# Second layer's heads: value products between pieces of projection, clamps and scalings on ScalarE

## What is computed

```
q, k, v, o, g, z = split(h @ w_in)              # per head: q, k 128 wide, v, o, z 256 wide
order = tril(ones)                              # a step sees itself and what came before
dmat  = where(order, b[t] - b[s] + ig[s], -inf) # b: running sum of log(sigmoid(forget gate))
m_t   = max over s of dmat (and of the state carried in)
s     = (q @ k.T) * exp(dmat - m_t)             # weights of one head, one direction
num, den = s @ v, sum(s)                        # and the state's part
h     = num / max(|den|, exp(-m_t))             # forward h + backward h
y     = rmsnorm(sigmoid(o) * (h_f + h_b)) * hn * silu(z)
out   = y @ w_out
```

## Time and profile before

| | |
|---|---|
| median of 3 runs | 2987.71 us (2981.6 to 2988.95) |
| profiled execution | 2990.57 us, its span 2988.8 us |
| granted TensorE clock, mean | 0.996 |
| TensorE busy | 2932.5 us, 98% |
| VectorE busy | 2090.1 us, 70% |
| ScalarE busy | 1178.0 us, 39% |
| GpSimd busy | 103.5 us, 3% |

### The profile page before, as it was taken

The page is one execution under the profiler, slowest core; times in us unless marked ns, Lnnn a source line. Parts: engine busy times, 40 slices in busy tenths (PEclk is TensorE's granted clock), DMA queues, the critical chain, the costliest instruction groups (busy, mean ns, idle before and its releaser), DMA issues.

```text
span 2988.8 us, 43582 instructions
## 1 busy us (share of the span) xinstructions
PE 2932.5 (98%) x17098; PEld 2353.5 (79%) x17098; DVE 2090.1 (70%) x3957; ACT 1178.0 (39%) x2056; POOL 103.5 (3%) x188
## 2 busy tenths in 40 slices
PE   8999999999999999999999999999999999999999
PEld 7777778888888888878888888888888888885346
DVE  4576876788888776677666886677675678765455
ACT  4322323322332232242245555455444445543344
POOL 0000000000000000000000000000010120000000
PEclk9999999999999999999999999999999999999999
DMA  9777784354555455538636774645576443487997
GB/s 366 281 266 286 273 282 149 127 169 148 190 168 177 162 183 169 179 128 275 235 117 206 258 241 142 197 148 180 195 236 218 141 164 128 152 274 259 403 404 314
DMA packets 193197, 641.69 MB, mean 215 GB/s; under 512 B 21488, under 2 KB 36192, under 8 KB 192992
## 3 DMA queue, kind: packets, MB, share of 16 engines
q1 hardware_dynamic: 132080, 423.44, 40.6%
q10 hardware_dynamic: 58032, 207.12, 20.3%
q0 software_dynamic: 2880, 8.35, 0.9%
HBM read 624.15 MB, written 12.58 MB: 213 GB/s over the span
## 4 chain that ended last, share of the span: by engine, by line
PE 87%; DVE 7%; ACT 3%; DMA 2%; issue 1%; SPq 0%; DVEq 0%; ACTq 0%; POOL 0%; POOLq 0%
PE PS L506 15%; PE PS L502 11%; PE PS L504 9%; PE PS L505 9%; PE PS L635 7%; PE PS L637 7%; PE PS L636 7%; PE PS L1061 2%; PE PS L798 2%; PE PS L1472 2%; DMA AR<-e_w 1%; DVE WL L2389 1%; PE PS L1441 1%; PE PS L1428 1%; PE PS L1122 1%
## 5 line engine op out<-in xcount | busy, mean ns | idle before, releaser
L2389 DVE TENSOR_TENSOR WL<-WR,WH 128x1024 fp32r<-128x1024 f32 (+1 forms) x566 | 682.4, 1211 | 401.7 <-ACT WH L1574 400.5
L506 PE MATMUL PS<-HT,WL 128*128 128x256 f32 (+1 forms) x2928 | 951.5, 325 | 0.0
L1574 ACT ACTIVATE WH<-WR 128x1024 fp32r<-128x1024 f32 (+1 forms) x566 | 587.1, 1044 | 873.1 <-PE PS L506 486.7
L506 PEld LDWEIGHTS PS<-HT,WL 128*128 128x128 f32 x2928 | 552.1, 189 | 47.6
L502 PE MATMUL PS<-HT,WH 128*128 128x512 f32 x1584 | 566.0, 401 | 9.2 <-DVE WL L2389 6.1
L504 PE MATMUL PS<-HT,WH 128*128 128x512 f32 (+1 forms) x1344 | 518.4, 386 | 5.4 <-DVE HT L2369 2.4
L505 PE MATMUL PS<-HT,WH 128*128 128x512 f32 (+1 forms) x1344 | 507.9, 378 | 0.0
L635 PE MATMUL PS<-WH,HT 128*128 128x512 f32 x1016 | 402.7, 396 | 3.5 <-DVE HT L2369 2.5
L637 PE MATMUL PS<-WH,HT 128*128 128x512 f32 x1016 | 396.8, 391 | 0.0
L636 PE MATMUL PS<-WL,HT 128*128 128x512 f32 x1016 | 396.2, 390 | 0.0
L502 PEld LDWEIGHTS PS<-HT,WH 128*128 128x128 f32 x1584 | 297.4, 188 | 90.2 <-issue 13.1
(11 more groups left out here) (472 smaller groups left out, 3319.1 us busy)
## 6 DMA issues: line engine op xcount, KB each, us to landing
WR<-ada_w SPq DMA_DIRECT2D x264, 512.0 KB, 4.6
AR<-e_w SPq DMA_DIRECT2D x88, 512.0 KB, 10.0
E_RING<-e_w SPq DMA_DIRECT2D x80, 512.0 KB, 10.2
WR<-m_vo ACTq DMA_DIRECT2D x64, 512.0 KB, 4.6
WR<-a_qz ACTq DMA_DIRECT2D x64, 512.0 KB, 4.8
WR<-n_m SPq DMA_DIRECT2D x64, 512.0 KB, 4.3
AR<-ada_p ACTq DMA_DIRECT2D x56, 512.0 KB, 6.3
AR<-ada_p SPq DMA_DIRECT2D x48, 512.0 KB, 8.0
```

The lines of the kernel that those rows point to most:

```text
L506: return e.matmul(ps[:, 0:b - a], wl, HH_[:, c, a:b], start=False, stop=c == last)
L1574: e.activation(part_of(WH, s), place_of(plan["slot"][p])[:, 0:width(s)], ACT.Copy, scale=1.0).then_inc(*L.up(hi_done, ("hi", s)))
L2389: e.tensor_tensor(part_of(WL, s), place_of(plan["slot"][plan["split"][s]])[:, 0:width(s)], part_of(WH, s).bitcast(F32), ALU.subtract).then ...
```

## The change

- TensorE: the value products of row block 0 now stand behind piece 0 of the next head's `vo`, those of block 1 behind piece 1, and so on to block 3; four pieces follow. Head 7 is left as it was.
- The weights: ScalarE takes `cb` from PSUM itself. The diagonal blocks (8 of 128 columns) it copies with the column added, GpSimd's `affine_select` then writes -3e38 where the order forbids, and eight exponentials of 128 columns follow; the rest (M_REST, 7 stretches, 1536 columns in all) goes through an exponential straight from PSUM. There is no clamp any more. VectorE multiplies only the stretches in M_BLOCKS.
- The scaling of d = 0 (four a head) and the four scalings at the end move from VectorE to ScalarE (`first_way`, `normed`).
- VectorE and ScalarE run the work after the value products step by step along `vo`: in step q the cut of a piece, for q < 4 the drain of block q, and one background block; in step 3 another background block stands behind the gate product.

```diff
@@ tables
+    M_REST = {(0, 0): [(128, 512)], (0, 1): [(256, 512)], (1, 0): [(256, 512)], (1, 1): [(0, 128), (256, 512)],
+              (2, 0): [(384, 512)], (2, 1): [], (3, 0): [], (3, 1): [(256, 384)]}
...
@@ TensorE
-            def vo(h):
-                tproject(("vo", h), I["m_vo"][h], 1, ALL, acc if h else wrk)
+            def vo(h, between=()):
+                tproject(("vo", h), I["m_vo"][h], 1, ALL, acc if h else wrk, between)
...
-                for tb in range(4):
+                def value_products(tb):
                     for d in range(2):
...
                 if h < 7:
-                    vo(h + 1)
+                    vo(h + 1, {tb: lambda tb=tb: value_products(tb) for tb in range(4)})
                 else:
+                    for tb in range(4):
+                        value_products(tb)
                     z_(h, 1)
@@ ScalarE
             for h in range(8):
+                if h:
+                    w.wait_ge(L.at(("p_used", h - 1)))
+                for d in range(2):
+                    ps, free = place[("cb", h, d)], ("free", ("cb", h, d))
+                    w.wait_ge(L.at(("full", ("cb", h, d))))
+                    for k in range(4):
+                        t = slice(128 * k, 128 * k + 128)
+                        e.activation(M_P[d][:, m_at(k, t.start, t.stop)], ps[:, t], ACT.Identity,
+                                     bias=M_ACOL[:, k, 32 * d + h:32 * d + h + 1], scale=1.0).then_inc(
+                            *L.up(act_done, ("pt", h, k, d), free))
+                    for k in range(4):
+                        for a, b in M_REST[k, d]:
+                            e.activation(M_P[d][:, m_at(k, a, b)], ps[:, a:b], ACT.Exp,
+                                         bias=M_ACOL[:, k, 32 * d + h:32 * d + h + 1], scale=1.0).then_inc(
+                                *L.up(act_done, ("pe", h, k, d), free))
                 for k in range(4):
-                    n = 512 if k < 2 else 256
                     for d in range(2):
-                        p = M_P[d][:, M_PC[k]:M_PC[k] + n]
-                        w.wait_ge(L.at(("pt", h, k, d)))
+                        p = M_P[d][:, m_at(k, 128 * k, 128 * k + 128)]
+                        w.wait_ge(L.at(("pa", h, k, d)))
                         e.activation(p, p, ACT.Exp, scale=1.0).then_inc(*L.up(act_done, ("pe", h, k, d)))
...
+                def first_way(tb):
...
+                    w.wait_ge(L.at(("pvs", h, tb, 0)))
+                    e.activation(M_HH[:, tb, :], place[("pv", h, tb, 0)][:, 0:256], ACT.Copy,
+                                 scale=M_ST[2 * tb % 4][:, 0:1]).then_inc(
+                        *L.up(act_done, ("pvx", h, tb), ("free", ("pv", h, tb, 0))))
...
                 if h < 7:
+                    for q in range(8):
+                        cut_to(plan[("vo", h + 1)][0] + q + NP)
+                        if q < 4:
+                            first_way(q)
+                        elif q == 4:
+                            squares()
+                        elif q == 5:
+                            normed()
                     vo(h + 1)
@@ VectorE
-                        ts(p, place[("cb", h, d)][:, c0:512], M_ACOL[:, k, 32 * d + h:32 * d + h + 1], 0.0,
-                           ALU.add, ALU.min, ("pt", h, k, d), *([("free", ("cb", h, d))] if k == 3 else []))
...
-                        if d == 0:
-                            scaled(M_HH[:, tb, :], ps[:, 0:256], s, ALU.mult, ("free", ("pv", h, tb, d)))
-                        else:
+                        recip(s, s, ("pvs", h, tb, d))
+                        if d:
+                            w.wait_ge(L.last(dve_done), L.at(("pvx", h, tb)))
...
                 if h < 7:
-                    bg(1)
...
-                    along_vo(h + 1, 0)
+                    for q in range(8):
+                        cut_to(plan[("vo", h + 1)][0] + q + NP)
+                        if q < 4:
+                            drained(q)
+                        if q == 3:
+                            opened()
+                            bg(1)
+                        elif q == 5:
+                            inverse()
+                        bg(1)
@@ GpSimd
-                        w.wait_ge(L.at(("pe", h, k, d)))
-                        e.affine_select(out=pd, in_=pd, compare_op=ALU.is_ge, fill=0.0, base=0,
+                        w.wait_ge(L.at(("pt", h, k, d)))
+                        e.affine_select(out=pd, in_=pd, compare_op=ALU.is_ge, fill=-3e38, base=0,
```

More of the change, by code:

```diff
@@ L1923, in mlstm @@
                 s = M_ST[h % 4]
[L1924 to L1930, removed]
@@ new lines, in squares @@
+                def squares():
+                    w.wait_ge(L.at(("yo", h), ("gated", 1, 2 * h + 1 if h < 7 else 14)))
+                    for tb in range(4):
+                        if tb >= 2:
+                            w.wait_ge(L.last(act_done))
+                        e.activation(M_E2[:, 256 * (tb % 2):256 * (tb % 2) + 256], M_HH[:, tb, :], ACT.Square, scale=1.0,
+                                     accum_out=s[:, 4 + tb:5 + tb]).then_inc(*L.up(act_done, ("ysq", h)))
+                    w.wait_ge(L.last(act_done))
+                    e.activation(s[:, 8:12], s[:, 4:8], ACT.Sqrt, bias=EPSC[:], scale=1.0 / 256).then_inc(
+                        *L.up(act_done, ("yr", h)))
@@ L1934, in mlstm @@
                     vo(h + 1)
                 else:
+                    for tb in range(4):
+                        first_way(tb)
+                    squares()
+                    normed()
                     z_(15)
@@ L2911, in mlstm @@
             w.wait_ge(L.at(("full", ("gt",))))
-            copy(SML[:, 0:320], place[("gt",)][:, 0:320], ("free", ("gt",)))
+            copy(SML[:, 0:320], place[("gt",)][:, 0:320], "columns", ("free", ("gt",)))
             w.wait_ge(L.last(dve_done))
             for h in range(8):
-                w.wait_ge(L.at(*(("full", ("cb", h, d)) for d in range(2))))
-                if h:
-                    w.wait_ge(L.at(("p_used", h - 1)))
                 for k in range(4):
@@ L2920, in mlstm @@
                     for d in range(2):
-                        p = M_P[d][:, M_PC[k]:M_PC[k] + 512 - c0]
-                        ts(p, place[("cb", h, d)][:, c0:512], M_ACOL[:, k, 32 * d + h:32 * d + h + 1], 0.0,
-                           ALU.add, ALU.min, ("pt", h, k, d), *([("free", ("cb", h, d))] if k == 3 else []))
[L2924 to L2929, removed]
+                        w.wait_ge(L.at(("pe", h, k, d), ("full", ("S", h, k))))
+                        for a, b in M_BLOCKS[k, d]:
+                            p = M_P[d][:, m_at(k, a, b)]
+                            tt(p, p, place[("S", h, k)][:, a - c0:b - c0], ALU.mult, ("p", h, k, d), ("free", ("S", h, k)))
                     if k == 0 and h:
@@ L2939, in mlstm, with drained @@
                         bg(2)
-                if h:
-                    w.wait_ge(L.at(("hh_used", h - 1)))
-                for tb in range(4):
+                st = M_ST[h % 4]
+                def drained(tb):
                     for d in range(2):
@@ L2969, in mlstm, with opened, inverse @@
-                if h < 7:
-                    along_vo(h + 1, 0)
-                else:
+                def opened():
+                    w.wait_ge(L.last(dve_done), L.at(("oe2", h)))
+                    tt(M_HH[:], M_HH[:], M_O[:], ALU.mult, ("yo", h), ("o_used", h))
+                def inverse():
+                    w.wait_ge(L.at(("yr", h)))
+                    recip(st[:, 8:12], st[:, 8:12], ("yi", h))
+                if h < 7:
+                    for q in range(8):
[8 more added lines that the diff above has]
+                        bg(1)
+                else:
+                    for tb in range(4):
+                        drained(tb)
+                    opened()
+                    inverse()
```

37 lines of the change are left out of this document (18 added, 19 removed).

## The result

The changed kernel takes 2994.08 us (median of 10 runs, 2990.23 to 2998.33), the kernel before 2987.98 in 10 runs beside it. The ratio is 1.0024, 95% interval 1.0015 to 1.0032: slower by 6.1 us between the medians, by 7.1 us between the means, which is the ratio's quarter of a per cent. The profiled execution has a span of 2993.9 us at a clock of 0.997.

What follows compares the result with a forecast made beforehand. TensorE, busy 98% of the span, was taken as the bound. Terms -4.3 + 6.8 + 2.8 = +5.3 us on the profiled 2990.6 gave 2995.9; with the runs' median 2.9 below, 2993, range 2991.5 to 2996.5 (0.48).

Steps and rivals of the forecast that it cites:

- The signs named beforehand: Traces: TensorE idle about 0.9 us before first value pieces; windows 5, 6 longer about 1 us, 0 to 3 by 0 to 2.
- The wait that goes: TensorE at the value products: five waits of 0.86 us for VectorE's drain of the first bank vanish, -4.3 us.
- The wait that comes: TensorE before the next values' first piece: waits for ScalarE's eviction of the keys, 0.97 us in seven heads, +6.8 us.
- Switching between the two kinds of products: TensorE changing between fp32 and fp32r products four times a head in place of once: 0 to 0.01 us each, 0.
- The turn: Between heads: VectorE and the next first score product come 0.7 us late in heads 0 to 3, +2.8 us.
- the wait for the load: VectorE before the turn: a background block's load, landing 4.6 us after issue, makes it wait 1.0 us.
- the bounds from 0 on: Lateness between heads by background-load landing: nothing at 3.6 us, 4.3 us late at 6.5; bounds 0 and +17 us.
- ScalarE's start of a head: Eight exponentials become 23 short instructions, 6.3 us on ScalarE, covered before TensorE wants the next piece: 0.
- that VectorE is in time at the turn: Rival: VectorE is not late between heads, +2.5 us, 2990.2 us; chance 0.21.
- the eviction hides: Rival: TensorE doesn't need the fourth bank so soon, so the keys' eviction costs nothing; -4.3 us, 2983.4; chance 0.06.
- the old wait stays: Rival: third value products still find their bank undrained, 0.86 us in five heads on top, 2997 us; chance 0.03.
- The background loads as the main cost: Rival: slow background-load landings delay VectorE between heads in four heads, slower by more than 9 us; chance 0.22.

Runs made afterwards that it cites:

- moves_alone: The changed kernel without the weave: all value products ahead of the next values' first piece, drained in one go; clamps and scalings stay off VectorE; 2987.39 us.
- weave_alone: The kernel before with value blocks 0 and 1 ahead of the first piece, 2 and 3 behind piece 1, drained stepwise; clamps and scalings on VectorE; 2982.67 us.
- first_ahead: The changed kernel with the value products of row block 0 ahead of the next values' first piece again, blocks 1 to 3 behind pieces 1 to 3; 2983.60 us.
- eviction_last: The changed kernel with TensorE's waits ahead of the first value piece reordered: low half and activations first, banks and keys' eviction last; 2989.15 us (one run).
- block_in_step2: The changed kernel with the background block behind step 3's product with the output gate moved into step 2 on VectorE; 2990.82 us.
- the four kernels with one order: Changed kernel, first_ahead, eviction_last and one taking banks when needed, all with the same VectorE order; turns late by 2.49, 1.72, 1.20 and 0.97 us.
- two_and_two: The changed kernel with value blocks 0 and 1 ahead of the next values' first piece, 2 and 3 behind piece 1; 2982.02 us.

## Why the prediction was right, point by point

The time was forecast at 2993.0 and is 2994.08; the stage was to lose 5.3 us and lost 7.1. That the time came closer than the stage is luck: the medians differ by 6.1 us, a figure that holds the scatter of the runs. The signs named beforehand came: heads 0 to 3, from the keys' last matmul to that of the next keys, are longer by 1.01, 1.33, 1.14 and 0.75 us, head 5 by 1.26.

- **The wait that goes** (-4.3): measured -4.1. Products and pieces of heads 0 to 4 took 53.09 us on average before, 52.27 in head 5 without the wait, which is 0.83 a head. moves_alone brings it back, weave_alone removes it without any of the moves: that VectorE's load a head is not the cause is shown; that the block in front of the first drain is, is read from both traces.
- **The wait that comes** (+6.8): the mechanism is right in place, releaser and count, and the term is 1.2 us too small. 0.97 us a head was made of the eviction, 0.06 from release to start, and 0.11 for a restart. Measured are 1.05 at the start, and the records behind it run slower: the stretch with four switches takes 52.48 us after this wait and 52.39 without it (first_ahead), 0.09 more. 1.14 x 7 = 8.0 us. What was mis-sized is the time from the release to the first matmul: the eviction ends at 733.67, the weights are loaded at 733.89, the matmul starts at 733.92. That is 0.25 us, where the value products started 0.06 after their release; eviction_last shows 0.11 of it to be the order of the waits. The rule of the Trainium skill that was weighed (TensorE: Matmul & The Clock Gate, section Step-by-step: what each phase is for) is of weight loads pulled ahead of matmuls that still run; the trace after again shows the load behind the wait, 0.22 us after the release.
- **Switching between the two kinds of products** (0): wrong in size. Four stretches in place of one cost 0.12 us a head (52.39 against 52.27), 0.8 in seven. The step took the first two records after one return alone, in head 1, which is a cheap one (0.01 us over twelve records); in head 5 of the same trace the return loses 0.05, and with four stretches 0.16 are lost in a head.
- **The turn** (+2.8): measured +2.5, in heads 0 to 3 and nowhere else, as said. Its parts were off against each other: the wait for the load was put at 1.0 us a head and was 0.65 in head 1 and 1.1 in all four together (between 745 and 785 us a load landed 4.3 us after its issue, by the median, where 4.6 had been reckoned). From the last products to the turned head 23.0 us had been reckoned and 23.1 were needed. That VectorE's work behind the last drain makes it is shown by block_in_step2; that the size hangs on the landings as well, as the bounds from 0 on said, is made likely by the four kernels with one order.
- **ScalarE's start of a head** (0): from the first biased copy, 787.70, to the end of the last exponential, 793.80, 6.1 us, 6.3 reckoned; TensorE's next piece starts at 801.21. TensorE does not wait for it. VectorE does, 1.80 us before it multiplies by the scores at 792.44, in time for TensorE. Three rows:

```profile
787.70 1.14 ACT L1928 ACTIVATE AR<-PS,SML 128x128 f32<-128x128 f32 x4
...
791.99 1.81 ACT L1940 ACTIVATE AR<-AR 128x128 f32<-128x128 f32 x8
793.59 1.15 ACT L1586 ACTIVATE WH<-WR 128x1024 fp32r<-128x1024 f32 x1
```

The sum in the stage: -4.1 + 8.0 + 0.8 + 2.5 - 0.1 (head 7) = 7.1. Two terms were too small by 2 us together, the median lies 1.1 over the forecast. The rivals: that VectorE is in time at the turn, that the eviction hides, and that the old wait stays are each excluded by a row above. The background loads as the main cost did not come, their waits stayed at 1.1 us in four heads. Two numbers of that rival do not follow from the prediction's own working: there a landing of 5.5 us makes the turn 2.2 us late, not 2.5 (+11.3 us), and the point of 9 us lies at 5.2, not 5.1.

## What to carry to other kernels

Before work is moved away from between two stretches of the busiest engine, ask what it covered there: the products had hidden the eviction of a bank that the next stretch asks for; 1.3 us of them left in place were enough, and so was asking for the bank only where it is written. Here the weave was worth the wait that it took away and nothing else; the engine that is late may be late by the order in its queue, so that 7 us less work a head on it change nothing. The end of the woven work matters as much as its start: whatever is drained last must leave the slower engine room until the next turn.

## What was not expected of the hardware

After the wait for ScalarE's eviction TensorE started its fp32r matmul 0.25 us behind the release, in all seven heads alike to 0.01, and 0.14 us with the waits in another order; fp32 products that waited for a drain started 0.06 behind VectorE's (before) and 0.05 behind ScalarE's (moves_alone: 733.82 to 733.87). The matmul stands behind three semaphores, the product behind one. What makes the rest of the difference, 0.08 us, was not tried and is open.

A return from fp32 to fp32r matmuls can cost more than its first two records show, up to 0.05 us, and not every time: 0.01 at the second return of two_and_two. Which one it is was not tried. With the weave the first matmul of a piece and the one after it lie 0.42 us apart in place of 0.23, but the first starts early for that (six products at 0.216 would last until 740.75, the piece starts at 740.56); what is lost, 0.04 us here, lies in some ten records behind, 0.231 apart on average in place of 0.227. The changed kernel, behind the first products of head 1:

```profile
739.45 1.46 PE L1070 MATMUL PS<-AR 128*128 128x257 f32 x6
740.56 0.58 PE L644 MATMUL PS<-WH,HT 128*128 128x512 f32 x1
740.98 0.39 PE L645 MATMUL PS<-WL,HT 128*128 128x512 f32 x1
```
